# A modulation vector by VectorE dot products instead of TensorE matmuls, and a norm moved in between units

## What is computed

```
cc  = silu(c)                                  # c: one vector of 1024 per sequence
mod = (cc @ w_ada + b_ada).reshape(b, 9, 1024) # w_ada: 1024 x 9216
sh1, sc1, gt1, sh2, sc2, gt2, sh3, sc3, gt3 = mod
h = rms_norm(x, g_ffn1) * (1 + sc1) + sh1      # modulated norm
x = x + 0.5 * gt1 * swiglu(h, w_ffn1_in, w_ffn1_out)
h = rms_norm(x, g_mix) * (1 + sc2) + sh2
x = x + gt2 * token_mix(h, ...)                # chunk attention and pooling, gated
h = rms_norm(x, g_ffn2) * (1 + sc3) + sh3
x = x + 0.5 * gt3 * swiglu(h, w_ffn2_in, w_ffn2_out)
```

## Time and profile before

| | us |
|---|---|
| median of 3 runs | 1809.2 (1808.81 to 1809.31) |
| span of the profiled execution, slowest core (core 0) | 1807.4 |
| spans of the 8 cores in it | 1795.6 to 1807.4 |
| modulation tiles 0 to 15 done | 55.6 |
| first unit of block 0 / of block 1 | 72.95 / 92.40 |
| end of group 0's units | 171.28 |
| PE busy from 171.3 to 690 (groups 1 to 4) | 507.3 of 518.7 |

### The profile page before, as it was taken

How to read it: one execution, slowest core, us unless ns; L and a number is a source line. 1 busy time by engine, 2 the same in 40 slices (tenths; PEclk the granted TensorE clock), 3 DMA queues, 4 the chain that set the end, 5 groups by cost and what they waited for, 6 DMA issues and landing times.

```text
span 1807.4 us, 23178 instructions; the slowest of 8 cores (1795.6 to 1807.4 us)
## 1 busy us (share of the span) xinstructions
PE 1624.6 (90%) x8431; PEld 799.0 (44%) x8568; DVE 753.6 (42%) x1074; ACT 500.4 (28%) x672; POOL 131.7 (7%) x159
## 2 busy tenths in 40 slices
PE   0588999999999994789999798999978999999998
PEld 0233444444444441356744346764433444444444
DVE  0344517144153154444434544443353625342515
ACT  1452010101101105545722374752253010111010
POOL 2000010110100100000011000001000000000000
PEclk9899999999999996898999998999988999999999
DMA  9946172563540442031046533016241431305025
GB/s 141 223 72 82 13 102 38 71 82 48 68 67 1 55 57 82 12 48 24 1 52 78 69 44 40 1 12 84 35 70 11 60 46 25 47 8 80 1 41 187
DMA packets 153742, 102.90 MB, mean 57 GB/s; under 512 B 11552, under 2 KB 138656, under 8 KB 153504
## 3 DMA queue, kind: packets, MB, share of 16 engines
q0 software_dynamic: 143792, 78.78, 34.2%
q1 hardware_dynamic: 9840, 22.64, 3.8%
HBM read 171.79 MB, written 8.39 MB: 100 GB/s over the span
## 4 chain that ended last, share of the span: by engine, by line
PE 79%; ACT 8%; issue 5%; DVE 4%; DMA 4%; ACTq 0%; DVEq 0%; POOL 0%; POOLq 0%
PE ps L598 19%; PE ps L510 18%; PE ps L517 18%; PE ps L835 3%; DMA arena<-w_ada 3%; PE ps L925 3%; PE ps L919 3%; PE ps L859 3%; PE ps L864 2%; PE ps L806 2%; PE ps L973 2%; PE ps L679 2%; PE ps L913 1%; ACT arena L768 1%; DVE arena L398 1%
## 5 line engine op out<-in xcount | busy, mean ns | idle before, releaser
L510 PE MATMUL ps<-arena 128*128 128x512 bf16 x1551 | 378.5, 386 | 37.2 <-DVE arena L406 26.6
L517 PE MATMUL ps<-arena 128*128 128x512 bf16 x1549 | 375.1, 382 | 1.8
L525 DVE TENSOR_TENSOR arena<-arena,ps 128x512 bf16<-128x512 bf16 x198 | 136.1, 688 | 531.2 <-PE ps L517 513.1
L598 PE MATMUL ps<-arena 128*128 128x512 bf16 x1551 | 341.4, 379 | 1.8
L522 ACT ACTIVATE arena<-ps 128x512 bf16<-128x512 f32 x198 | 117.8, 596 | 771.6 <-PE ps L510 768.2
L605 DVE SCALAR_TENSOR_TENSOR arena<-ps,arena 128x512 f32<-128x512 f32 x360 | 270.2, 751 | 81.5 <-PE ps L598 50.3
L510 PEld LDWEIGHTS ps<-arena 128*128 128x128 bf16 x1584 | 153.8, 99 | 225.1 <-issue 51.3
L517 PEld LDWEIGHTS ps<-arena 128*128 128x128 bf16 x1584 | 156.5, 99 | 191.8 <-issue 8.6
L598 PEld LDWEIGHTS ps<-arena 128*128 128x128 bf16 x1584 | 154.8, 98 | 186.7
L840 ACT ACTIVATE arena<-ps 128x1536 bf16<-128x1536 f32 x64 | 92.6, 1451 | 43.4 <-PE ps L835 42.6
L843 DVE TENSOR_TENSOR arena<-arena 128x1536 bf16<-128x1536 bf16 x64 | 61.4, 959 | 75.1 <-ACT arena L840 75.1
(11 more groups left out here) (86 smaller groups left out, 1182.0 us busy)
## 6 DMA issues: line engine op xcount, KB each, us to landing
arena<-w_ada POOLq DMA_DIRECT2D x36, 512.0 KB, 7.4
arena<-w_in POOLq DMA_DIRECT2D x32, 512.0 KB, 9.3
arena<-xT SPq DMA_DIRECT2D x5, 2048.0 KB, 15.0
arena<-w1i POOLq DMA_DIRECT2D x20, 512.0 KB, 13.4
arena<-w3i POOLq DMA_DIRECT2D x20, 512.0 KB, 7.4
outT<-arena SPq DMA_DIRECT2D x16, 512.0 KB, 3.6
arena<-w1o POOLq DMA_DIRECT2D x5, 1024.0 KB, 13.7
arena<-w3o POOLq DMA_DIRECT2D x5, 1024.0 KB, 11.2
```

The lines of the kernel that those rows point to most:

```text
L510: ins = e.matmul(bank(ba), lhsT=wa[:, kt, jj * 128:(jj + 1) * 128], rhs=hb[:, kt, :], start=(kt == 0), stop=(kt == 7))
L517: ins = e.matmul(bank(bb), lhsT=wb[:, kt, jj * 128:(jj + 1) * 128], rhs=hb[:, kt, :], start=(kt == 0), stop=(kt == 7))
L525: S.op("dve", lambda e: e.tensor_tensor(out=actb(jl, b), in0=SA[i % 2][:, :], in1=bank(bb), op=ALU.mult), reads=[SAR[i % 2], BANK[bb]], wr ...
L598: ins = e.matmul(bank(ob + dn), lhsT=lw, rhs=actb(jl, b), start=(jl == 0), stop=(jl == nk - 1))
```

## The change

`w_ada` is laid out anew by the host: 72 tiles of 128 output features (partitions) by 1024 inputs, each contiguous, 4 KB for a partition. A tile is loaded as fp32, without a cast, by SP's hardware queue (`ada_tile`), and `ada_dot` multiplies it on DVE with silu(c), held as bf16 on all partitions (`CCB`, made on ACT from a loaded broadcast of c, `crow`), and sums along the row into one column of MOD. Ten buffers take the first ten tiles; tiles 10 to 15 reuse them as the dots of 0 to 5 are done. Tiles from 16 on use two of the buffers, a dot behind each unit from the fourth to the eleventh (unit numbers 3 to 10), and then behind each unit with an even number. The loads of the first weights of the feed-forward wait for tile 11. Only block 0 is normed before the first unit. The norm of block b+1 now runs inside the four units of block b: square after the first, statistics after the second, four apply steps after the third and four after the fourth.

```diff
+    CROW = view(o_w + 4096 * 9, F32, (D,))
+    S.op("sp", lambda e: e.dma_start(out=CROW[:, :], in_=crow), writes=[WP[9]], dma="d_crow")
+    S.op("act", lambda e: e.activation(out=CCB[:, :], in_=CROW[:, :], func=AF.Silu), reads=[WP[9]], writes=[CCBR])
...
-    def ada_chunk(c):
...
-            for jj in range(2):
-                j = 2 * c + jj
-                for kt in range(8):
-                    ins = e.matmul(MODPS[part][:, j:j + 1], lhsT=wt[:, kt, jj * 128:(jj + 1) * 128],
-                                   rhs=SCB[:, kt:kt + 1], start=(kt == 0), stop=(kt == 7))
...
+    ASLOT = [(o_w + 4096 * i, WP[i], "d_a%d" % i) for i in range(4, 9)] + \
+            [(o_actb + 4096 * i, Res(), "d_as%d" % i) for i in range(5)]
+    def ada_tile(j, k):
+        o, res, key = ASLOT[k]
+        wt = view(o, F32, (D,))
+        ADA_DMA[j] = S.op("sp", lambda e: e.dma_start(out=wt[:, :], in_=w_ada[:, j * D:(j + 1) * D]),
+                          writes=[res], dma=key, nobar=True)
+        ADA_TILE[j] = (wt, res)
+    def ada_dot(j):
+        wt, res = ADA_TILE[j]
+        S.op("dve", lambda e: e.scalar_tensor_tensor(
+            out=wt[:, :], in0=wt[:, :], scalar=1.0, in1=CCB[:, :],
+            op0=ALU.mult, op1=ALU.mult, accum_out=MOD[:, j:j + 1]),
+            reads=[res, CCBR, CSTR], writes=[res, MODR], nobar=True)
...
-    for c in range(8):
-        ada_chunk(c)
-    mod_finish(0, 0, 16, [0, 1])
+    for j in range(10):
+        ada_tile(j, j)
+    for j in range(16):
+        ada_dot(j)
+        if j < 6:
+            ada_tile(10 + j, j)
+    mod_finish([0, 1])
     S.op("sp", lambda e: e.dma_start(out=xblk(1), in_=xv[:, :, TB:2 * TB]),
-         writes=[XR[1]], dma="d_x1", deps=[ADA_DMA[5]])
+         writes=[XR[1]], dma="d_x1")
...
-                 writes=[WP[0]], dma="d_w0", nobar=True)
+                 writes=[WP[0]], dma="d_w0", nobar=True, deps=[ADA_DMA[11]])
...
-            norm_seq([nitem(pending_norms.pop(0)), nitem(pending_norms.pop(0))], sub, SQ_F, RSTD, TMP, 6)
+            n0 = [nitem(pending_norms.pop(0))]
+            if not first:
+                n0.append(nitem(pending_norms.pop(0)))
+            norm_seq(n0, sub, SQ_F, RSTD, TMP, 6)
...
-            if ada_next[0] < 36 and ((ada_next[0] < 12 and i >= 8) or (ada_next[0] >= 12 and i % 3 == 2)):
-                ada_chunk(ada_next[0])
+            if ada_next[0] < 72 and i >= 3 and (ada_next[0] < 24 or i % 2 == 0):
+                j = ada_next[0]
+                while ada_issued[0] < min(72, j + 2):
+                    ada_tile(ada_issued[0], ada_issued[0] % 2)
+                    ada_issued[0] += 1
+                ada_dot(j)
                 ada_next[0] += 1
...
+                            if first:
+                                if u == 1 and pending_norms:
+                                    nth_ = norm_thunks([nitem(pending_norms.pop(0))], sub, SQ_F, RSTD, TMP, 6, False)[0]
+                                    nth_[0]()
+                                elif u == 2 and nth_:
+                                    nth_[1]()
+                                    nth_[2]()
+                                elif u >= 3 and nth_:
+                                    for t in nth_[3 + 4 * (u - 3):7 + 4 * (u - 3)]:
+                                        t()
+                                    if u == 4:
+                                        nth_ = []
+                                continue
```

More of the change, by code:

```diff
@@ L128, in build_nc @@
     cst_d = din("cst", [128, NCST])
-    w_ada = din("w_ada", [D, 9 * D])
+    w_ada = din("w_ada", [128, 72 * D])
+    crow = din("crow", [128, D])
     w1i = din("w1i", [D, 2 * DFF])
@@ L179, in build_nc @@
     DER = view(o_der, F32, (9, 8))
-    o_scb = alloc(8 * 2)
-    SCB = view(o_scb, BF16, (8,))
     o_ones = alloc(128 * 2)
@@ L216, in build_nc @@
     WOX = [view(o_sqf + 5120, BF16, (1024,)), view(alloc(2048), BF16, (1024,))]
+    CCB = view(alloc(D * 2), BF16, (D,))
     ffn_end = off[0]
@@ L252, in build_nc @@
     VIEWS = dict(XB=XB, HALO=HALO, H=H, MOD=MOD, DER=DER, CST=CST, ACTB=ACTB, H2=H2, KT=KT, V=V, QT=QT, YP=YP,
-                 EXPB=EXPB, ATT=ATT, MRG=MRG, MIXED=MIXED, SCB=SCB)
+                 EXPB=EXPB, ATT=ATT, MRG=MRG, MIXED=MIXED)
     def check(name):
@@ L287, in build_nc @@
                                            scalar2=None, op0=ALU.mult), reads=[CSTR, MISC], writes=[MISC])
-    S.op("act", lambda e: e.activation(out=SCB[:, :], in_=CST[:, 0:8], func=AF.Silu), reads=[CSTR], writes=[MISC])
+    CROW = view(o_w + 4096 * 9, F32, (D,))
+    CCBR = Res()
+    S.op("sp", lambda e: e.dma_start(out=CROW[:, :], in_=crow), writes=[WP[9]], dma="d_crow")
+    S.op("act", lambda e: e.activation(out=CCB[:, :], in_=CROW[:, :], func=AF.Silu), reads=[WP[9]], writes=[CCBR])
     S.op("pool", lambda e: e.dma_start(out=WPG[:, :, :], in_=w_pg.rearrange("(g c) d -> c g d", c=128)),
@@ L290, in build_nc @@
          writes=[MISC], dma="d_wpg", nobar=True)
-    ada_v = w_ada.rearrange("(k p) n -> p k n", p=128)
-    MODPS = [bank(7), bank(7)]
-    MODBANK = [BANK[7], BANK[7]]
+    ASLOT = [(o_w + 4096 * i, WP[i], "d_a%d" % i) for i in range(4, 9)] + \
+            [(o_actb + 4096 * i, Res(), "d_as%d" % i) for i in range(5)]
     ADA_DMA = {}
-    def ada_chunk(c):
[L299 to L306, removed]
-            for jj in range(2):
-                j = 2 * c + jj
-                for kt in range(8):
-                    ins = e.matmul(MODPS[part][:, j:j + 1], lhsT=wt[:, kt, jj * 128:(jj + 1) * 128],
-                                   rhs=SCB[:, kt:kt + 1], start=(kt == 0), stop=(kt == 7))
-            return ins
-        S.op("pe", mm, reads=[WP[piece], MISC], writes=[MODBANK[part]], nobar=True)
@@ L315, in mod_finish @@
-    def mod_finish(part, lo, hi, rows):
-        S.op("dve", lambda e: e.tensor_tensor(out=MOD[:, lo:hi], in0=MODPS[part][:, lo:hi], in1=CST[:, 8 + lo:8 + hi],
-                                               op=ALU.add), reads=[MODBANK[part], CSTR], writes=[MODR], nobar=True)
+    def ada_tile(j, k):
[4 more added lines that the diff above has]
+        ADA_TILE[j] = (wt, res)
@@ new lines, in build_nc, with mod_finish @@
+    ADA_TILE = {}
+    def ada_dot(j):
[4 more added lines that the diff above has]
+            reads=[res, CCBR, CSTR], writes=[res, MODR], nobar=True)
+    def mod_finish(rows):
+        lo, hi = 8 * rows[0], 8 * rows[-1] + 8
+        S.op("dve", lambda e: e.tensor_tensor(out=MOD[:, lo:hi], in0=MOD[:, lo:hi], in1=CST[:, 8 + lo:8 + hi],
+                                               op=ALU.add), reads=[MODR, CSTR], writes=[MODR], nobar=True)
@@ L472, in ffn @@
         cnt = [0]
-        ada_next = [8] if first else [36]
+        ada_next = [16] if first else [72]
+        ada_issued = [16]
         GSIZES = [4, 4, 4, 5, 5]
@@ L528, in unit @@
                 deps=([NRES["sq"].w] + list(NRES["sq"].r.values())) if jl == 4 else ())
-            if ada_next[0] < 36 and ((ada_next[0] < 12 and i >= 8) or (ada_next[0] >= 12 and i % 3 == 2)):
-                ada_chunk(ada_next[0])
+            if ada_next[0] < 72 and i >= 3 and (ada_next[0] < 24 or i % 2 == 0):
[4 more added lines that the diff above has]
+                ada_dot(j)
                 ada_next[0] += 1
[L532 to L535, removed]
+                if j == 23:
+                    mod_finish([2])
+                if j == 71:
+                    mod_finish([3, 4, 5, 6, 7, 8])
         for g in range(ngroups):
@@ L1048, in _prep @@
     shared = {
-        "w_ada": np.ascontiguousarray(f("w_ada")[0]),
+        "w_ada": np.ascontiguousarray(f("w_ada")[0].T.reshape(72, 128, D).transpose(1, 0, 2).reshape(128, 72 * D)),
         "w1i": np.ascontiguousarray(f("w_ffn1_in")[0]),
@@ L1088, in _prep @@
         m["cst"] = cst
+        m["crow"] = np.ascontiguousarray(np.broadcast_to(c[b], (128, D)))
         in_maps.append(m)
```

## The result

The changed kernel takes 1831.45 us (1829.24 to 1831.6, 4 runs) against 1809.26 us for the kernel before on the same chip: ratio 1.0116, 95% interval 1.0101 to 1.0131. It is slower by 22 us, where 7 were forecast and 1826 was the range's end. The profiled execution spans 1829.9 us on its slowest core, core 1, against 1807.4 us on core 0.

A forecast was written before the change was run, and what follows sets the result against it. Loads bound the start, the norm's ACT and DVE chain the hand-overs, PE the full stretch. From 1807.4 us, -6.7 (term A), +22.4 (Term B) and -9.0 (Term C) gave 1814.1, with 1.8 added 1816; range 1805 to 1826.

The forecast's parts named there:

- Term B: Group 0, block 1 to the projection: each norm compressed into one block, plus dots, makes 78.9 us into 101.25; +22.4 us.
- Term C: Full stretch from 171 us on: 22 chunks of line 310 matmuls leave PE, 0.41 us each; -9.0 us.
- term A: Start up to block 1: first unit at 50.6 us, block 1 at 85.7 instead of 92.40; -6.7 us.
- tiles or weights come so late that block 1 starts no earlier than now: Rival on the start's loads: block 1 starts no earlier than 92.4 us, total 1823 us; chance 0.09.
- Cheaper loads: Rival on tile loads: cost per packet, 93.5 ns for 4 KB, block 1 at 73, total 1803 us; chance 0.08.
- The full clock: Rival at block starts: clock stays full, first units 3.45 us instead of 6.0, total 1806 us; chance 0.13.
- The double dot: Rival on DVE: a dot costs 2.3 us instead of 1.25 (halved rate), total 1825 us; chance 0.10.

The follow-up runs named there:

- e3: The kernel before with only the norm's move, no dots and no uncast tiles: ratio 1.0104, two executions at 1827.7 and 1828.3 us.
- e2: The changed kernel with the norm's move undone, dots, tiles and loads as changed: ratio 0.9958, 1801.4 us.
- e1: The changed kernel with the load of group 0's output weights (w1o) held back until unit 11's mult: ratio 1.0069, 1822.0 us.
- e8: The kernel before with 32 bytes added, so that later buffers stand off a multiple of 64 bytes: ratio 0.9997.
- e6: e2 with w1o held back, tiles 16 and 17 loaded ahead of x2, and 32 bytes of padding: ratio 0.9936, 1799.3 us.
- e7: The changed kernel with 32 bytes of padding, putting later buffers back on the addresses of the kernel before: ratio 1.0160.
- e5: The changed kernel with each unit's dot put behind that unit's apply steps instead of ahead: ratio 1.0021, 1813.4 us.
- e9: e6 with three carried apply steps behind each unit instead of two, dots from unit 12, one behind every unit from 101: ratio 0.9988, unclear.
- e11: e6 with three carried apply steps behind each unit instead of two, dots from unit 3 on: ratio 0.9917.

## Why the prediction was wrong in size

**What held.** The direction, and the mechanism step by step. Block 0's first unit came at 54.5 (50.6 forecast). Block 1's start was set by the end of the chain that was named: dot 16 waiting for tile 16, then four apply steps. Term B: from block 1 to the projection 99.4 us against 101.25 forecast, the starts 28.97, 27.63 and 26.72 apart against 28.95, 28.25 and 27.7; PE stood still for 9 to 10 us each time (11 forecast) and began at the low clock each time. That the first distance fits to 0.02 us is luck: PE's own work took 18.6 us for 18.1, the stall 10.35 for 10.85. Between the changed kernel and the one before term B is +20.5 for +22.4. e3 shows that it is the norm's move: alone, it costs 19 us (ratio 1.0104). Undone, in e2, it gives back 29 (by the ratios, 1.0116 and 0.9958); that is more than term B, because dot 16's wait then no longer stands ahead of a norm that the next block needs at once. Term C: from the end of group 0's units to that of the feed-forward 506.4 us against 515.4, the -9.0 that were forecast. These are the rows of the last projection on PE in both kernels:

```profile
643.32 43.33 PE L598 MATMUL ps<-arena 128*128 128x512 bf16 x196
```

```profile
661.10 43.33 PE L624 MATMUL ps<-arena 128*128 128x512 bf16 x200
```

They end at 686.65 and 704.43.

**The step that failed** is term A, "and tile 16, behind x4 on SP's queue, at 80": it was there at 93.0, so that block 1 began at 98.7 instead of 85.7 and term A was +6.3 instead of -6.7. Against the span the forecast fell short by 15.8 us: 13.0 of term A, 4.7 behind the first feed-forward (below), less 1.9 by which term B came out cheaper. The list of what shares the DMA engines before tile 16 left out w1o. The chunks of `w_ada` did not only take POOL's queue themselves; each waited for PE, and so held back everything behind it. Taking them off the queue moved w1o from 133 to 42 us, and the forecast had put it at nothing. e1 prices it at 8 to 9 us in the mean over the cores, in which dot 16 started at 94.4, 14 us late.

Most of the rest are the first sixteen tiles: the last dot of them began at 43.82 instead of 40 (in the mean over the cores at 44.8). They were late from the start. The earlier trace rows were read as x0 being there at 11.5 us; but bytes moved by 12 us don't say that a load has landed, and in the kernel before the square of block 0 waited for x0 until 14.30. In the changed kernel crow came at 15.34 instead of 13 and the first dot began at 19.21. ACT in the kernel before, then ACT and DVE in the changed one:

```profile
14.30 3.62 ACT L344 ACTIVATE arena<-arena 128x4096 bf16<-128x4096 f32 x1 [8.71 <-DMA arena<-xT]
```

```profile
15.34 1.28 ACT L291 ACT_TABLE_LOAD   x1 [15.34 <-DMA arena<-crow]
```

```profile
19.21 1.23 DVE L310 SCALAR_TENSOR_TENSOR arena<-arena 128x1024 f32<-128x1024 f32 x1 [15.15 <-DMA arena<-w_ada]
```

What remains, 1 to 2 us in the mean, lies somewhere in x1 to x4 beside the weights and is not taken apart. A weight packet alone was priced at 68 to 70 ns, while the earlier trace rows give 65.8 (97.3% of 16 x 28 us over 6622), so that price was not too low. The prediction named the outcome as a rival ("tiles or weights come so late that block 1 starts no earlier than now", 1823), with 0.09; "For it: tile 16 stands behind 8 MB of x" was the right thought, but 2 MB of w1o went beside them, and block 1 started not at 92.4 but at 98.7.

**What was not forecast at all** is the stretch behind the first feed-forward, 1114.7 us in the mean over the cores against 1109.9, with the same instructions. PE is not near its limit there, other than the section on the time before says: from 690 to 1795 us it is busy 1015.28 of 1105 us on core 0 of the kernel before, so waits can count. The three kernels without dots took 1109.9, 1109.1 and 1109.1 (before, e8, e3), those with dots 1109.7 to 1114.7 (e6 lowest). Within it waits of PE for w_po and w_ao were 3.8 us in the mean against 1.5, and the granted clock 0.956 against 0.959; but e8 has 3.0 us of these waits and 1109.1. It isn't the 32 bytes (e7, e8), and e6 at 1109.7 speaks against the dots. Whether it is a spread between executions or an effect stays open; it accounts for up to 5 of the 22 us.

**The rivals.** Cheaper loads fell: in this kernel 1953 packets of mostly 4 KB took 96.0% of 16 x 23 us, 181 ns each, so the cost is by bytes, as taken (DMA queues of the changed kernel from 12 to 35 us):

```profile
q1 hardware_dynamic: 1953, 7.09, 96.0%
```

The full clock fell: all five block starts show matmuls of 3.57 us for eight. The double dot fell: a dot is 1.23 us and its accumulator read 0.08, and from one dot to the next with no wait it is 1.34 us (22.46 to 23.80, in DVE's timeline below). The Trainium skill, VectorE: DVE Perf Modes, says in its section on two Vector instructions with no wait between them that an operation which also writes out its accumulator is two instructions; the trace agrees, the second being the DVE_READ_ACCUMULATOR of 0.08 us. The estimate with that rule was 1.4 us and the one without it 1.25. The Trainium skill, Vector Engine (DVE) Microarchitecture Reference, says in its list of points that are easy to get wrong that this instruction runs at half rate with two sources that are not bf16; with one bf16 source the rate was not halved, and no run here has two fp32 sources with an accumulator.

```profile
22.46 1.23 DVE L310 SCALAR_TENSOR_TENSOR arena<-arena 128x1024 f32<-128x1024 f32 x1
23.61 0.08 DVE L310 DVE_READ_ACCUMULATOR arena<-arena 128x1 f32 x1
23.80 1.23 DVE L310 SCALAR_TENSOR_TENSOR arena<-arena 128x1024 f32<-128x1024 f32 x1
```

## What to carry to other kernels

When operations leave an in-order queue, list what stood behind them and when it is now free to start: here a 2 MB load came 91 us earlier, into the stretch in which the units waited for loads, and cost 8 to 9 us. A norm whose statistics, table loads and apply steps all stand within the block right ahead of its use costs a stall and a low clock at every hand-over (19 us here by itself). Starting it one block earlier, in e2, made the first unit 11 us later and the whole 29 us shorter. An operation that waits for a load belongs behind the work that others wait for on its engine: in e5, moving the dot behind four apply steps gave back 17 us.

## What the runs showed of the hardware that was not expected

The third of three loads of x issued in a row kept SP's queue busy for 13.4 us in the changed kernel (9.2 in the one before), so tile 16 was not even issued until 73.2 us. With w1o held back, in e1, the three took 9.2 us in all and tile 16 was issued at 68.2. SP in the changed kernel, the three loads of x and then tile 16 with the two behind it:

```profile
58.27 14.84 SPq L457 DMA_DIRECT2D arena<-xT  x3
73.21 21.45 SPq L302 DMA_DIRECT2D arena<-w_ada  x3
```

In e5 (1827.8 us, once), e7, e9 and e11 two or four cores took some 15 to 25 us longer than the others in some executions of the same program: 0 and 1, 2 and 3, or 6 and 7 together. The traces of e9 and e11 show where: a granted clock of 0.81, between the two levels, for some 160 us from the end of group 0 on, while cores beside them have the full clock. What brings it on is not shown.
